# Score tiles and turned token rows of a sample block moved between the V sums of the blocks ahead of it

## The reference

```
q = (hb @ w_q)                      # 128 tokens, 8 heads x 2 sides x 128
s = einsum('thsk,snk->thsn', q, sub_keys)      # scores against 2 x 128 keys
top_s, top_i = top_k(s, 16)         # per head and side
cand = top_s[..., 0, :, None] + top_s[..., 1, None, :]
best_s, best_j = top_k(cand, 16)    # 16 experts per head, 128 per token
gate = softmax(best_s)
act = gelu(einsum('thkd,td->thk', u_tab[idx], hb))
out = einsum('thk,thkd->td', gate * act, v_tab[idx])
```

## Time and profile before

| | |
|---|---|
| median of 3 runs | 4969.91 us (4968.59 to 4973.04) |
| the profiled execution | 4967.69 us, its span 4965.9 us |
| PE busy | 3861.3 us, 78% |
| DVE busy | 3242.6 us, 65% |
| POOL busy | 1447.9 us, 29% |
| ACT busy | 748.0 us, 15% |
| gathers, DMA queue q0 | 1342.26 MB, 67.4% of 16 engines |
| POOL idle ahead of L634 until a score matmul (L891) of PE | 138.9 us in 3 waits |
| mean granted TensorE clock | 0.93 |

### The profile page before, as it was taken

How to read it: one execution, slowest core, us unless ns; L and a number is a source line. 1 busy time by engine, 2 the same in 40 slices (tenths; PEclk the granted TensorE clock), 3 DMA queues, 4 the chain that set the end, 5 groups by cost and what they waited for, 6 DMA issues and landing times. The chain is left out here.

```text
span 4965.9 us, 36487 instructions
## 1 busy us (share of the span) xinstructions
PE 3861.3 (78%) x11046; PEld 1898.0 (38%) x11046; DVE 3242.6 (65%) x8263; ACT 748.0 (15%) x2211; POOL 1447.9 (29%) x1284
## 2 busy tenths in 40 slices
PE   7588678988777776788868786788977687777776
PEld 6464334643222222235535443346422222222222
DVE  1546765536887868854574766664378787687666
ACT  0111124211101010010121112341010100100101
POOL 0001112212454434432222021221044354354432
PEclk9788788999999999999989897899999999999999
DMA  8334456754998999999969254566389899899998
GB/s 266 99 116 178 153 188 242 252 194 192 412 415 368 421 374 414 421 390 387 365 245 366 97 203 146 206 253 220 127 354 421 365 419 421 362 421 421 407 421 341
DMA packets 342149, 1497.72 MB, mean 302 GB/s; under 512 B 31424, under 2 KB 176448, under 8 KB 178112
## 3 DMA queue, kind: packets, MB, share of 16 engines
q0 software_dynamic: 184320, 1342.26, 67.4%
q1 hardware_dynamic: 157632, 153.13, 9.6%
HBM read 1491.97 MB, written 3.31 MB: 301 GB/s over the span
## 5 line engine op out<-in xcount | busy, mean ns | idle before, releaser
L680 PE MATMUL expert_acc<-uv_ring,diag 128*128 128x512 f32 x3744 | 1865.1, 631 | 417.9 <-DVE diag L1227 407.8
L634 POOL DMA_INDIRECT uv_ring<-uv,expert_index x936 | 1050.2, 1122 | 2717.1 <-PE expert_acc L680 2174.4
L680 PEld LDWEIGHTS expert_acc<-uv_ring,diag 128*128 128x128 f32 x3744 | 688.1, 198 | 1487.8 <-DVE diag L1227 898.5
L1218 DVE CUSTOM_DVE_ANT_0 uv_ring<-uv_ring,arena 128x1024 f32<-128x1024 f32 x680 | 831.5, 1223 | 243.2 <-DMA uv_ring<-uv,expert_index 240.5
L680 PE MATMUL expert_acc<-arena,diag 128*128 128x512 f32 x1376 | 687.8, 632 | 264.2 <-DVE diag L1227 196.3
L951 ACT ACTIVATE gelu<-u_dot 128x1 f32<-128x1 f32 x1280 | 256.0, 203 | 2943.8 <-DVE u_dot L1218 2943.2
L1227 DVE TENSOR_SCALAR diag<-const_mats,expert_gate,gelu 128x128 f32<-128x128 f32 x1280 | 465.7, 364 | 308.8 <-ACT gelu L951 214.1
L634 POOL DMA_INDIRECT arena<-uv,expert_index x344 | 397.6, 1156 | 757.2 <-PE expert_acc L680 460.3
L1218 DVE CUSTOM_DVE_ANT_0 arena<-arena 128x1024 f32<-128x1024 f32 x344 | 420.8, 1223 | 172.6 <-DMA arena<-uv,expert_index 171.2
L680 PEld LDWEIGHTS expert_acc<-arena,diag 128*128 128x128 f32 x1376 | 243.4, 195 | 698.1 <-DVE diag L1227 425.2
L1218 DVE CUSTOM_DVE_ANT_0 uv_ring<-uv_ring,prompt_rows 128x1024 f32<-128x1024 f32 x256 | 312.1, 1219 | 113.4 <-DMA uv_ring<-uv,expert_index 112.9
(11 more groups left out here) (202 smaller groups left out, 2785.0 us busy)
## 6 DMA issues: line engine op xcount, KB each, us to landing
w_ring<-w_ada SPq DMA_DIRECT2D x66, 512.0 KB, 11.3
w_ring<-w_in SPq DMA_DIRECT2D x64, 512.0 KB, 5.0
w_ring<-w_pq SPq DMA_DIRECT2D x64, 512.0 KB, 4.5
w_ring<-w_out SPq DMA_DIRECT2D x32, 512.0 KB, 6.3
uv_ring<-w_ada SPq DMA_DIRECT2D x30, 512.0 KB, 5.3
uv_ring<-uv,expert_index POOLq DMA_INDIRECT x936, 11.7
arena<-b_ada SPq DMA_DIRECT2D x48, 128.0 KB, 6.2
arena<-uv,expert_index POOLq DMA_INDIRECT x344, 15.7
```

Of the source, the lines that this page charges most:

```text
L634: pool.indirect_dma_start(out=UV[j], out_offset=None, in_=uv, in_offset=bass.IndirectOffsetOnAxis(ap=idxs[:, n % 2, k:k + 1], axis=0)).the ...
L680: ins = pe.matmul(acc[:, half, :], diag[:, m % DIAGS, :], UV[SLOT_AT[m]][:, D + 512 * half:D + 512 * half + 512], start=(k == 0), stop=(k ...
L1218: V_.tensor_tensor_reduce(UV[j][:, 0:D], UV[j][:, 0:D], rows_of(n), 1.0, 0.0, ALU.mult, ALU.add, dots[:, m % DOTS:m % DOTS + 1]).then_inc( ...
```

## The change

`score_block` is split into `turn_rows` (one ht tile) and `score` (one ps tile), ACT's `drain_scores` likewise. Ahead of block 0's V sums only block 1's four ps tiles stay. A new function says what stands after slot k of block b: the two ht tiles of block b+1 after slots 8 and 9, the four ps tiles of block b+2 after slots 124 to 127. PE places each tile after the V sum of that slot, ACT each copy after the gelu of that slot. The order of tiles in PSUM follows. DVE waits for the token rows at slot 0 of a block instead of ahead of it. Nothing is computed differently.

```
+ROWS_AT, SCORES_AT = 8, 124
+def turned_at(g, b, k):
+    nb = GROUP_BLOCKS[g]
+    if b + 1 < nb and ROWS_AT <= k < ROWS_AT + 2:
+        return ("ht", b + 1, k - ROWS_AT)
+    if b + 2 < nb and SCORES_AT <= k < SCORES_AT + 4:
+        return ("ps", b + 2, k - SCORES_AT)
+    return None
...
# psum_order
-            for b in range(1, nb):
-                out += [("ht", l, g, 2 * b), ("ht", l, g, 2 * b + 1)]
-                out += [("ps", l, g, 4 * b + i) for i in range(4)]
+            if g:
+                out += [("ps", l, g, 4 + i) for i in range(4)]
+                for x in (turned_at(g, b, k) for b in range(nb) for k in range(SLOTS)):
+                    if x is not None:
+                        out.append((x[0], l, g, (2 if x[0] == "ht" else 4) * x[1] + x[2]))
...
# PE
-                    for b in range(nb):
-                        if b + 1 < nb:
-                            score_block(b + 1)
+                    for k in range(4):
+                        score(1, k)
+                    for b in range(nb):
...
                         for k in range(SLOTS):
                             add_v(n, k)
+                            turned = turned_at(g, b, k)
+                            if turned is not None:
+                                (turn_rows if turned[0] == "ht" else score)(*turned[1:])
...
# ACT
-                        if 0 < b < nb - 1:
-                            drain_scores(b + 1)
...
                             gelu(n, k)
                             if b == 0 and k == SECOND_AT:
                                 gate_exp(1, slice(HALF, PH))
-                                drain_scores(1)
+                                for i in range(4):
+                                    drain_scores(1, i)
...
+                            turned = turned_at(g, b, k)
+                            if turned is not None:
+                                (drain_rows if turned[0] == "ht" else drain_scores)(*turned[1:])
...
# DVE
-                        dve.wait_ge(*free["ht"].at(l, g, 2 * b + 1))
+                        if b == 0:
+                            dve.wait_ge(*free["ht"].at(l, g, 1))
...
                         for k in range(SLOTS):
+                            if b and k == 0:
+                                dve.wait_ge(*free["ht"].at(l, g, 2 * b + 1))
                             dot(n, k)
```

More of the change, by code:

```diff
@@ L880, in _, with turn_rows, score @@
                     pe.wait_ge(*free["n2"].at(l, g, 2 * nb - 1))
[L881 to L893, removed]
+                    def turn_rows(b, half):
+                        t = fill("ht", l, g, 2 * b + half)
+                        for c in range(4):
+                            ins = turn(t[:, c * P:(c + 1) * P], hT[:, 4 * half + c, b * P:(b + 1) * P])
+                        done(ins, "ht")
+                    def score(b, k):
+                        t = fill("ps", l, g, 4 * b + k)
+                        for m in range(4):
+                            ins = pe.matmul(t[:, m * P:(m + 1) * P], qT[:, b, 4 * k + m, :],
+                                            keys[:, m % 2, :], start=True, stop=True)
+                        done(ins, "ps")
                     for u in range(PQ_UNITS):
@@ L905, in _ @@
                             pe.wait_ge(*free["pq"].at(l, g, 7))
-                            score_block(0, 0, 2)
+                            for half in range(2):
+                                turn_rows(0, half)
+                            for k in range(2):
+                                score(0, k)
                     pe.wait_ge(*free["pq"].at(l, g, 15))
-                    score_block(0, 2, 4)
+                    for k in range(2, 4):
+                        score(0, k)
                     beside.rest()
@@ L1117, in _, with drain_rows, drain_scores @@
                     act.wait_ge(*free["n2"].at(l, g, 2 * nb - 1))
[L1118 to L1128, removed]
+                    def drain_rows(b, half):
+                        t = tile_of("ht", l, g, 2 * b + half)
+                        if b >= 2 and half == 0:
+                            act.wait_ge(s_dot, (blk(l, g, b) - 1) * SLOTS)
+                        nc.scalar.activation((htok[b % 2] if g else htok_p[:])[:, 512 * half:512 * half + 512], t, ACT.Copy).then_inc(free["ht"].sem, 1)
+                    def drain_scores(b, k):
+                        t = tile_of("ps", l, g, 4 * b + k)
+                        if b and k == 0:
+                            act.wait_ge(*s_idx.at(l, g, 2 * b - 1))
+                        nc.scalar.activation(scs[:, 4 * k:4 * k + 4, :].rearrange("p s n -> p (s n)"), t, ACT.Copy).then_inc(free["ps"].sem, 1)
                     def gate_exp(i, heads=slice(0, PH), l=l, g=g):
@@ L1138, in _ @@
                         if i == 7:
-                            drain_scores(0, 0, 2)
-                    drain_scores(0, 2, 4)
+                            for half in range(2):
+                                drain_rows(0, half)
+                            for k in range(2):
+                                drain_scores(0, k)
+                    for k in range(2, 4):
+                        drain_scores(0, k)
                     beside.rest()
```

## The result

| | median | runs | lowest to highest |
|---|---|---|---|
| before | 4976.23 us | 13 | 4968.59 to 4980.81 |
| changed | 4990.32 us | 13 | 4982.68 to 4995.77 |

The ratio is 1.0028 with a 95% interval of 1.0020 to 1.0037, that is +14.1 us (10 to 18). The forecast was +12.4 us, 0.25%. The forecast time of 4982.3 lies 8.0 under the measured median, and the range, up to 4990.0, misses it by 0.3: the median of before, 4969.9 over three runs when the forecast was made, is 4976.2 over thirteen. One run of before, beside the later experiments, took 5369 us at a granted clock of 0.72 and stands in no number here.

A forecast was written before the change was run, and what follows sets the result against it. The prediction took the gathers to bound sample blocks, with a pause at four block changes until POOL restarts. Score tiles 11.1 plus turned rows 1.3 made +12.4 us on the 4969.9 median: 4982.3 us, range 4972 to 4990.

The forecast's parts named there:

- What bounds the kernel: Sample blocks last as long as their gathers; at four block changes gathers pause until POOL restarts after the last score tile.
- Part 1: Block change, last V sum to POOL's first gather: 7.21 us becomes 3.54, a gain of 3.67 at each of four places.
- Part 2: Slots 124 to 127: gelu waits behind ACT's copy, V sums step 4.20 us instead of 1.84; with part 1, +11.1 us.
- the fourth place: Last block change of layer 1: V sums already slowed 1.47 us by half clock; 1.98 to 3.45 later, middle 2.7 taken.
- Part 3: The two turned tiles moved from ahead of block 0 to its slots 8 and 9: (a) and (b) together +1.3 us.
- (b): Slots 8 and 9 of block 0: the same closed chain delays slot 10's weighting, a loss of 3.03 us over both layers.
- (a): Ahead of block 0: POOL no longer waits for the eight transposes, a gain of 0.87 us per layer, 1.74.
- The sum: Whole kernel: 11.1 + 1.3 = 12.4 us slower, put onto the median of 4969.9, giving 4982.3 us.
- The tiles hide in the slots: Rival at slots 124 to 127: V sums keep a step under 3.27 us, 16.4 us less, 4953.5; chance 0.06.
- Set by something else: Rival: stream doesn't wait for POOL's restart, or gain and loss come out alike; 4970 to 4979 us; chance 0.30.
- The clock: Rival: TensorE falls to half clock for the whole chain, 8 us per place, 32 in all, about 5014; chance 0.04.

The follow-up runs named there:

- e5: Changed kernel with all four score tiles on PE after slots 100 to 103, ACT's copies still after 124 to 127; ratio to before 0.9900.
- e4: Changed kernel with the turned rows at slots 40 and 41 instead of 8 and 9, score tiles unmoved; ratio to before 1.0023.
- e2: Changed kernel with score tiles on PE still after 124 to 127 but ACT's four copies all after slot 127; ratio to before 0.9994.
- e3: Changed kernel with score tiles on PE after slots 100, 101, 102 and 127, ACT's copies still after 124 to 127; ratio to before 0.9973.
- e1: Changed kernel with all four score tiles and their copies after slot 127, turned rows still at 8 and 9; ratio to before 0.9993.
- e7: Changed kernel with score tiles and ACT's copies together at slots 116 to 119, turned rows still at 8 and 9; ratio to before 0.9892.

## Why the prediction was right in its mechanism and missed in its time

**What bounds the kernel.** Right. The gathers set a sample block, and the pause at the change of block is real time: taking it away in e5 took 49.1 us out of the stretches, of 52.2 that the four pauses hold beyond the usual 2.5 each.

**Part 1, what goes behind the last V sum.** 3.54 forecast for V sum 127 to POOL, 3.65 measured. Gain 3.56 per place instead of 3.67.

**Part 2, the chain.** 4.20 forecast, 4.11 measured: 1.82 to the score matmul and 1.10 to the copy as in the rows of before, 0.49 for the copy instead of 0.57 (the low end of its bounds), 0.30 and 0.40 as before. The half clock fell into it once in the first profile, not at the fourth place, where the sum had half of 1.47 for it, but at the first:

```profile
1515.47 5.40 PE L694 MATMUL expert_acc<-uv_ring,diag 128*128 128x512 f32 x8 [2.54 <-DVE diag L1257]
...
1522.99 1.98 PE L694 MATMUL expert_acc<-uv_ring,diag 128*128 128x512 f32 x4 [1.23 <-DVE diag L1257]
```

Two V sums take 5.40 there against 3.82 at the same slots of block 1; the wait that PE had before them, 2.54, is the same at both. In the two repetitions of the changed kernel it fell into none of the eight places, in e4 into two of four. The rule of the Trainium skill (PSUM — Partial Sum Buffer, Engine vs sequencer instructions) that ScalarE's queue is strict FIFO is what the rows show: the gelu at 1860.80 had its input at 1858.48, before the copy at 1860.31 began, and still runs behind it, and e2, with the copies behind the gelus, has no 4.1 step.

Over the three profiles of each kernel the four pauses together are 71.2 us on average, changed, against 62.2 before, so +9.0 where +11.1 was forecast. From V sum 124 to POOL's first gather the changed kernel takes 15.96 to 15.98 us (16.14 forecast) at eleven of twelve places and 16.87 at the one with the half clock. Part of the difference is in the kernel before: the forecast took its 13.51, 13.24, 13.24 and 14.16 from one profile, and its two repetitions have 13.25 to 14.22, at a granted clock below 1 at six of eight places. Another part is the fourth place, where 2.7 was forecast and 15.97 - 14.16 = 1.8 came.

**Part 3, the turned rows.** (b) From V sum 8 to the weighting of slot 10 the rows of after give 6.96 where 7.02 was forecast:

```profile
1220.24 1.98 PE L694 MATMUL expert_acc<-arena,diag 128*128 128x512 f32 x4 [0.63 <-DVE diag L1257]
...
1227.20 0.35 DVE L1257 TENSOR_SCALAR diag<-const_mats,expert_gate,gelu 128x128 f32<-128x128 f32 x1 [0.80 <-ACT gelu L973]
```

and the DMA share of the windows above is 0.89 and 0.86, where the kernel before has 0.92 in both at the same distance from its first gather. +3.0 was forecast; the stretches leave 11.8 - 9.0 = 2.8 for this and all else inside the blocks, and e4, with the rows elsewhere, has -0.9. (a) is right too, though not in the whole time, which varies by more: POOL's wait ahead of the first gather of sample block 0 is 93.53 us in layer 0 of all three executions of before and 92.66 in those of the changed kernel, 0.87 less, and as much less in layer 1.

**The sum.** For the stretches 11.1 + 3.0 = 14.1 was forecast and 11.8 measured; for the whole +12.4 was forecast and +14.1 timed, with an interval of 10 to 18. The term mis-sized within the stretches is the pause, by 2 us. That the whole came so near is in part luck: 11.8 for the stretches and 1.7 less ahead of them make 10.1, at the low end of that interval, and the other 4 us, no more than that interval reaches to either side, have no place in the kernel that the runs show.

**The step that failed** is the one after the sum: "the difference goes onto the median: 4969.9 + 12.4", and with it the range. Three runs of before had a median of 4969.9; thirteen have 4976.2, and twenty-five and nine more, beside the experiments, 4977.1 and 4975.2. 4976.2 + 12.4 = 4988.6 would have been 1.7 under the measured median. The upper bound of 4990 was made of bounds of the change's own terms (+19.2) and of nothing for the base, as if 4968.6 to 4973.0 were all that this kernel does.

It was more than bad luck with three draws from thirteen. Those three are the three lowest of the thirteen (the next is 4974.97), and the changed kernel's first three on record are low as well: their median is 4982.8, 12.9 above that of before's first three and 0.5 from the forecast time. The ten later runs of each have medians of 4976.7 and 4991.6. So both kernels ran 7 to 9 us slower in the later runs, the difference changed little, and what differed between the earlier and the later runs isn't on record.

For one part of the kernel it can be shown where the time moves from one execution to another. In all thirteen profiled executions the code ahead of sample block 0 in layer 0 is the same but for those 0.87 us, and POOL's first gather there starts anywhere from 1182.6 to 1193.9. The two ends, e3 first, with the window of the stage ahead of it:

```profile
1182.62 0.94 POOL L643 DMA_INDIRECT arena<-uv,expert_index  x1 [92.66 <-PE rotating L901]
...
0.00:1180.00 1180.00, 916.14 (x3373) 573.49 (x3373) 632.71 (x1774) 233.59 (x544) 141.42 (x132) 0.89 0.52 179
```

then e1:

```profile
1193.91 0.94 POOL L643 DMA_INDIRECT arena<-uv,expert_index  x1 [92.66 <-PE rotating L901]
...
0.00:1180.00 1180.00, 922.18 (x3324) 577.54 (x3325) 632.83 (x1774) 230.00 (x540) 137.95 (x132) 0.87 0.52 179
```

DVE's work is equal; PE's granted clock is 0.89 and 0.87. Added up from the clock's own records, the time at half clock (1.2 GHz) ahead of block 0 is 266 us in e3 and 311 in e1, and over the thirteen executions it goes with that start at a correlation of 0.95, 0.28 us later per us at half clock. For the stage between the stretches the correlation is weaker, 0.55 over a spread of 13 us, so what else moves that one stays open. That the half clock makes the stage long, and not the other way round, is argued and wasn't tried.

**The rivals.** "The tiles hide in the slots" asked for a step under 3.27; it is 4.11. e2 with 2.6 and e7 with another place show it right about the room and wrong about the order. "Set by something else" had two halves: that the stream doesn't wait for POOL's restart is refuted by e5, and that gain and loss come out alike by the 11.8 us of the stretches. "The clock" for the whole chain: it fell into one step at one place of the twelve in the three profiles of the changed kernel, not into all. What the prediction held against it was misread: the gap of 1.3 us in steady slots is that of the weight loads, and PE's own gap there is 0.5, where the chain's is 1.23, so the rows of before didn't tell.

## What to carry to other kernels

Ask of a moved step whose program it enters, not whose time it fills: a copy of half a microsecond on an engine that is 15% busy made the step 2.3 us longer per slot, because an instruction that the critical chain wants stood behind it in order. Separate the producer from the copy: let PE fill PSUM early, where another engine's wait (here POOL's) depends on the read being over, and let ACT empty it where it is free. And where the wait is for the last of several tiles, moving three of four gives a quarter of what moving all four gives. Before a forecast of a few tenths of a percent is put onto a median of three, allow for the spread of the untouched stages, and for runs taken at another time, as well.

## What the runs showed that was not expected

Counted by its packets, the last gather ahead of a pause seems to land late: 3.9 to 7.5 us after the one before it instead of 2.49, at all four places of ten executions with a pause, and at 2.5 in e5, where a gather is queued behind it. It isn't late. A gather counts its semaphore up sixteen times, and the last count is what DVE waits for. For the gather of slot 127 of sample block 1 in the kernel before, the records have the first count at 1847.95, the fifteenth at 1850.04 and the sixteenth at 1852.72 (DVE's dot product of that slot begins at 1852.74), and for the gather ahead of it the sixteenth at 1850.23, 2.49 us earlier. Wherever both gathers have all their counts on record, the last one ahead of a pause ends 2.5 to 2.8 us after the one before it. What the packets show is that one share of sixteen runs behind the others: in e2 the counts of one gather lie 1.2 us apart at the start of block 1 and 5.6 at its end, and in e5, without a pause, those of slot 127 lie 5.9 apart as well (1842.40 to 1848.31). While the queue is full the next gather's packets hide it. Why one share falls behind stays open.

And a stage with the same code varied by 11 us from one execution to another, and what moved with it in its windows was the granted clock.
